# Turning attention probabilities in 32x32 blocks on VectorE, value products on four groups of 32 rows, and units of four heads

## The reference, cut to what matters

```
def sparse_attend(q, k_sel, v_sel, valid):
    s = einsum('btngd,btknd->btngk', q, k_sel) * (B_HD ** -0.5)
    s = where(valid, s, -inf)
    p = softmax(s, axis=-1)
    return einsum('btngk,btknd->btngd', p, v_sel)
```

## Time and profile before

| | us |
|---|---|
| median of three runs (lowest, highest) | 4006.8 (4002.0, 4010.1) |
| span of the profiled execution, first to last instruction | 4000.7 |
| phase of the change, first product to last copy | 2202 to 3035 |
| of it blocks 0 to 5 | 2202 to 2412 |
| of it blocks 6 to 11 | 2412 to 2749 |
| of it blocks 12 to 15 | 2749 to 3035 |

### The profile page before, as it was taken

One profiled execution on the slowest core, in us unless ns is written; L12 is line 12 of the kernel. 1 busy time (PEld: TensorE's weight loads), 2 busy tenths in 40 slices (PEclk: granted clock), 3 DMA queues, 4 the chain that ended last, 5 costly groups with the idle time before them and its releaser, 6 DMA issues. The chain is left out here.

```text
span 4000.7 us, 41769 instructions
## 1 busy us (share of the span) xinstructions
PE 3854.3 (96%) x14518; PEld 2310.1 (58%) x14518; DVE 2916.5 (73%) x3866; ACT 1411.3 (35%) x2593; POOL 1672.7 (42%) x1529
## 2 busy tenths in 40 slices
PE   7899999999999999999999799999997999999999
PEld 4555555564456566665665566555553788854444
DVE  5589999689999999999996566555454577653333
ACT  5411211155334423433431666555553322111121
POOL 0000045459687656665654332122103766552111
PEclk9999999999999999999999899999997999999999
DMA  6312222420111121211211633232232855531111
GB/s 221 92 60 65 67 87 86 142 95 37 61 61 68 50 71 64 71 63 66 72 58 59 194 120 99 70 88 77 61 102 87 226 168 171 169 128 69 40 53 46
DMA packets 290039, 368.31 MB, mean 92 GB/s; under 512 B 72635, under 2 KB 217619, under 8 KB 286630
## 3 DMA queue, kind: packets, MB, share of 16 engines
q1 hardware_dynamic: 249434, 249.73, 20.7%
q0 software_dynamic: 19664, 86.31, 5.9%
q10 hardware_dynamic: 20736, 29.66, 2.3%
HBM read 235.04 MB, written 129.28 MB: 91 GB/s over the span
## 5 line engine op out<-in xcount | busy, mean ns | idle before, releaser
L1315 DVE MAX8 best<-score 128x8 f32<-128x384 f32 (+13 forms) x448 | 639.7, 1428 | 23.3 <-POOL score L1283 8.3
L1317 DVE MATCH_REPLACE8 score<-best,score 128x384 f32<-128x384 f32 (+13 forms) x448 | 631.2, 1409 | 0.0
L1072 PE MATMUL pr<-xnT,w_row 128*128 128x347 f32 (+1 forms) x960 | 298.3, 457 | 0.0
L1224 POOL TENSOR_TENSOR kT<-kT 128x347 f32<-128x347 f32 (+1 forms) x240 | 193.8, 808 | 215.2 <-ACT kT L1142 208.4
L396 PE MATMUL pg<-xnT,wt 128*128 128x416 f32 x800 | 281.8, 515 | 0.0
L1700 PE MATMUL mix_slot<-mix_kT,mix_bq 128*128 128x512 f32 (+3 forms) x640 | 271.6, 540 | 7.7 <-DVE mix_sd L2039 3.2
L1739 PE MATMUL mix_po<-mix_probT,mix_v 128*128 128x512 f32 x544 | 240.4, 595 | 5.2 <-ACT mix_probT L1839 4.3
L1072 PEld LDWEIGHTS pr<-xnT,w_row 128*128 128x128 f32 x960 | 180.3, 190 | 106.6 <-issue 10.0
L1142 ACT COPY kT<-pr 128x347 f32<-128x347 f32 (+1 forms) x240 | 106.7, 446 | 352.9 <-PE pr L1072 342.5
L396 PEld LDWEIGHTS pg<-xnT,wt 128*128 128x128 f32 x800 | 152.6, 191 | 127.6 <-issue 127.6
L1224 POOL TENSOR_TENSOR kT<-kT,sm 128x347 f32<-128x347 f32 (+1 forms) x179 | 159.7, 892 | 124.7 <-ACT sm L1142 121.7
(11 more groups left out here) (636 smaller groups left out, 8048.0 us busy)
## 6 DMA issues: line engine op xcount, KB each, us to landing
gt_scr<-kT SPq DMA_DIRECT2D x40, 694.0 KB, 3.3
out_gm<-gt_scr ACTq DMA_DIRECT2D x32, 520.0 KB, 5.3
gt_scr<-kT SPq DMA_DIRECT2D x20, 692.0 KB, 4.2
wt<-in_w_in SPq DMA_DIRECT2D x22, 512.0 KB, 4.0
w0a<-in_w_in SPq DMA_DIRECT2D x11, 1024.0 KB, 6.6
w_row<-in_w_in SPq DMA_DIRECT2D x10, 1024.0 KB, 6.7
qt_scr<-kT POOLq DMA_DIRECT2D x8, 1040.0 KB, 4.3
early<-ybt_scr SPq DMA_DIRECT2D x4, 2080.0 KB, 9.5
```

The source lines that it names most:

```text
L1072: ins = nc.tensor.matmul(pr[:, b, 0:w], lhs, rhs, start=k == 0, stop=k == 3)
L1224: nc.gpsimd.tensor_tensor(o[:, slot, :], o[:, slot, :], term, ALU.add).then_inc(added, 1)
L1315: nc.vector.max(best[:, :], sc).then_inc(top_step, 1)
L1317: nc.vector.match_replace(sc, best[:, :], sc, TAKEN).then_inc(top_step, 1)
```

## The change

The order of the work becomes `MIX_UNITS`: 32 units of four heads (one group of keys and values) and one block, first all 16 blocks of group 0, then all 16 of group 1. Unit u has block i = u mod 16. Probabilities of several units lie in a ring of 8 x 2048 columns (`mix_ring`, `ring_places`). The events change in these ways:

- **T** is gone. A new event **X** lets DVE turn a head in blocks of 32x32 within groups of 32 rows (`nc.vector.transpose`, STREAM_TRANSPOSE). **N** leaves the reciprocal on DVE and moves the scaling to ACT.
- **O** becomes `values_times_probs`: for each 32 keys, four products of 32 rows by 128 columns, one for each group of 32 rows, each into its own bank of `mix_po` (four banks). Each product has its own weights, 32 rows of values; so the values lie in memory four times, once in each group of 32 rows (`load_values`, four transfers). There are 16(i+1) products in a unit, 4352 in all, in place of 272 of 512 columns and 1088 turns.
- PSUM: three slots of one bank in place of two slots of two and two banks for turns. Score pieces have up to 512 columns, 320 in place of 192; M2, M3 and M4 take one slot for each head; the turned keys become an event MT with a slot.
- `memory_steps` spreads the memory tile m over heads 8m-4 to 8m+3. A unit with odd i begins with M1 and MT, then M2 in two heads, then half of M3; a unit with even i has the other half of M3, M4 with Q, M4, and Y.
- The turns and products of a unit follow a unit or two later: `products(u)` turns up to unit u+1 if it is scored, then multiplies unit u. It is called when more than `ahead` units wait, or when the next unit needs ring space that a waiting one holds.
- Keys and values of group 1 are loaded in the middle of the phase, and queries and masks for every unit.

```
+        while turned <= min(u + 1, scored):
+            events.extend(("X", GQ * turned + h) for h in range(GQ))
+            turned += 1
+        events.append(("O", u))
+    scored = -1
+    for u, (kv, i) in enumerate(MIX_UNITS):
+        ahead = 2 if u == 0 or 0 < i < 6 else 1
+        while waiting and (waiting[0] <= after[u] or len(waiting) > ahead):
+            products(waiting.pop(0))
+        for h in range(GQ):
+            n = GQ * u + h
+            events.append(("S", n, 0))
+            events += memory.get(n, [])
+            if n in sample:
+                events.append(sample[n])
+            events += [("S", n, q) for q in range(1, key_pieces(n))]
+            events.append(("E", n))
+            if h:
+                events.append(("N", n - 1))
+        events.append(("N", n))
...
+                for b in range(blocks):
+                    for a in range(QUADS):
+                        rows = slice(BLK * a, BLK * a + BLK)
+                        ins = mm(po[:, a, 0:GQ * BLK], v[rows, b, :], at[rows, :, BLK * b:BLK * b + BLK], start=b == 0, stop=b == blocks - 1)
...
+                elif kind == "N":
+                    act.wait_ge(inverse, i + 1)
+                    nc.scalar.activation(probs(i), probs(i), ACT.Copy, scale=rsum[:, i % RECENT:i % RECENT + 1]).then_inc(normed, 1)
...
+                    dve.wait_ge(p_ready, i + 1)
+                    if i >= RECENT:
+                        dve.wait_ge(normed, i - RECENT + 1)
+                    nc.vector.reciprocal(rsum[:, r:r + 1], sums[:, r:r + 1]).then_inc(inverse, 1)
+                elif kind == "X":
+                    dve.wait_ge(normed, i + 1)
+                    nc.vector.transpose(probs(i), probs(i)).then_inc(turned, 1)
```

More of the change, by code:

```diff
@@ L1349, in step, with head_width, key_pieces, ring_places @@
         return 1
-def key_pieces(i):
-    return len(pieces((i + 1) * P))
-def key_groups(i):
-    return -(-(i + 1) // 4)
+GQ = BH // KV
+MIX_UNITS = [(kv, i) for kv in range(KV) for i in range(NB)]
+MIX_HEADS = GQ * len(MIX_UNITS)
+BLK = 32
+QUADS = P // BLK
+RING_COLS = 8 * SEQ
+RECENT = 8
+SLOTS = 3
 FIRST_SAMPLE_STEP = 12
 FIRST_KEYS = 4
+def head_width(n):
+    return (MIX_UNITS[n // GQ][1] + 1) * P
+def key_pieces(n):
+    return len(pieces(head_width(n), 512))
+def ring_places():
+    at, after, cursor = [], [], 0
+    for u, (_, i) in enumerate(MIX_UNITS):
+        size = GQ * (i + 1) * P
+        if cursor + size > RING_COLS:
+            cursor = 0
+        shared = [w for w in range(u) if at[w] < cursor + size and cursor < at[w] + GQ * (MIX_UNITS[w][1] + 1) * P]
+        at.append(cursor)
+        after.append(max(shared, default=-1))
+        cursor += size
+    return at, after
 def sample_events():
@@ new lines, in memory_steps @@
+def memory_steps():
+    tile = lambda m: [[("M1", m), ("MT", m)], [("M2", m, 0), ("M2", m, 1)], [("M2", m, 2), ("M2", m, 3)],
+                      [("M3", m, 0), ("M3", m, 1)], [("M3", m, 2), ("M3", m, 3)], [("M4", m, 0), ("M4", m, 1), ("Q", m)],
+                      [("M4", m, 2), ("M4", m, 3)], [("Y", m)]]
+    first = tile(0)
+    at = {n: first[2 * n] + first[2 * n + 1] for n in range(4)}
+    for m in range(1, NB):
+        for x, step in enumerate(tile(m)):
+            at[8 * m - 4 + x] = step
+    at[8 * NB - 4], at[8 * NB - 3] = [("L", 0)], [("L", 1)]
+    return at
@@ new lines, in mixing_events, with products @@
+def mixing_events():
+    sample, memory = sample_events(), memory_steps()
+    assert max(sample) < MIX_HEADS and max(memory) < MIX_HEADS
+    _, after = ring_places()
+    events, waiting, turned = [], [], 0
+    def products(u):
+        nonlocal turned
+        while turned <= min(u + 1, scored):
[18 more added lines that the diff above has]
+        events.append(("N", n))
+        waiting.append(u)
+        scored = u
+    for u in waiting:
+        products(u)
@@ L1691, in score_piece @@
             def score_piece(e):
-                _, i, hd, q = e
-                p = i % 2
-                if hd == 0 and q == 0:
-                    pe.wait_ge(a_loaded[p], 32 * (i // 2 + 1))
-                    pe.wait_ge(k_resident[i >= FIRST_KEYS], 16)
-                lo, width = pieces((i + 1) * P)[q]
-                s = take_slot(e)
-                for a, m in pieces(width, 512):
-                    ins = mm(slot[:, s, a:a + m], bq[p][:, hd, :], kT[:, hd // 4, lo + a:lo + a + m], start=True, stop=True)
@@ L1701, in score_piece @@
[L1701 to L1722 removed]
+                _, n, q = e
@@ L1922, in _ @@
                     act.wait_ge(rden_ready, i + 1)
-                    after_slot(act, ("M3", i, 0))
-                    after_slot(act, ("M3", i, 1))
+                    for hh in range(AH):
+                        after_slot(act, ("M3", i, hh))
                     for hh in range(AH):
```

414 lines of the change are left out of this document (182 added, 232 removed).

## The result

The changed kernel takes 4096.3 us (median of 4 runs, 4091.8 to 4098.4), the kernel before 4004.4 in the same comparison: a ratio of 1.0227, with a 95% interval of 1.0212 to 1.0241. It is slower by 92 us. I had forecast 4016, 9 us above the 4006.8 of its three runs then, with a range up to 4090: the sign was right and the size was not, and the time lies outside the range.

What follows compares the result with a forecast made beforehand. TensorE was taken as the bound, its order hiding the others. Blocks 0 to 5, 6 to 11 and 12 to 15 summed 179+310+353 = 842 us against 833: forecast 4016 us, 0.2% slower, range 3950 to 4090.

Steps and rivals of the forecast that it cites:

- Work that leaves and comes: TensorE: value records and turns (355 us) leave, tiled products (242) and form changes (11) come; net 102 us less.
- The other ends: Dearer prices for a set of four products on TensorE: 0.145 us (sum 73 us longer) or 0.43 (+700 us).
- The turn and the scaling: VectorE's turn 2.3 us at 2048 columns, 2.16 at 1920; ScalarE's scaling 2.01 at 2048; neither engine becomes the bound.
- Waits in the widest blocks: Blocks 12 to 15, both groups: TensorE waits 97 us in score phases and ahead of products; 353 us against 286.
- Blocks 6 to 11: Both groups: own work 281 us, waits 21 for slots and VectorE's load, 8 for gathers and drains; 310 against 337.
- Blocks 0 to 5: Both groups: own work 152 us, the 27 us of waits kept, extra value copies included in that; 179 against 210.
- The clock mis-sized: TensorE's clock drops at eight idle stretches of 7 to 12 us, 1.5 us each, 12 us in all.
- Rival 1: Waits in units 12 to 15 smaller, 55 us for 97, and 15 less elsewhere: 3950 us; chance 0.21.
- rival 2: VectorE's turn or the tiled products dearer: 4085 us at twice the turn, 4089 at 0.145 a set; chance 0.24.

Runs made afterwards that it cites:

- x6: Changed kernel with each unit placed in the ring where the latest reader is earliest, wide units at the two ends in turn: 4020.9 us.
- x2: Changed kernel with the values loaded once, in one transfer of 128 partitions, a quarter of the bytes (products read wrong blocks): 4057.1 us.
- x5: Changed kernel with all four copies kept, the rest of the values loaded two key blocks at a time behind the loads of the next units: 4069.4 us.
- x11: Changed kernel with the same four value transfers and bytes, each filling 128 partitions of a quarter of the places (products read other keys' values): 4073.5 us.
- x4: Changed kernel without the memory tiles' loads from tile 2 on, except the decay row (memory steps work on old data): 4069.6 us.
- x7: Changed kernel with a memory tile's three loads issued at three places in place of one burst, same bytes: 4064.6 us.
- x8: Changed kernel with the edits of x5, x6 and x7 together: 3968.0 us, ratio 0.9899 to the kernel before.
- x9: x8 with the sample step C moved behind its head's scores and exponential: 3953.0 us, ratio 0.9873 to the kernel before.

## Why the prediction missed, step by step

By thirds of the phase, the sum's terms and what they measured (us: length = work at full speed + idle + clock's price; the scores of units 16 and 17, which stand ahead of O15, are counted to blocks 0 to 5):

| blocks | my sum | measured |
|---|---|---|
| 0 to 5 | 179 = 152 + 27 + 0 | 267 = 170 + 73 + 23 |
| 6 to 11 | 310 = 281 + 29 + 0 | 296 = 258 + 29 + 9 |
| 12 to 15 | 353 = 249 + 92 + 12 | 359 = 250 + 86 + 24 |

**Work that leaves and comes: right.** Eight records, two for each of the four row groups, take 0.224 us in runs at the full clock, (6.53-0.27)/223 x 8 in the one below, 0.112 a set; I had 0.111.

```profile
2365.32 6.53 PE L1773 MATMUL mix_po<-mix_ring,mix_v 32*128 32x128 f32 x224
```

In sum it fell by 97 us where I had said 102; between the blocks some 20 us of it stand earlier than I had put them. The other ends that I had weighed, 0.145 and 0.43 a set, are out. The Trainium skill's factor for four row groups ("TensorE: Matmul & The Clock Gate", Part 3, Measured speedup vs the span model), 3.07, is given there for 512 columns; for the 128 columns here this trace shows more: a product of 32 rows alone would take the 0.112 of a 128-column record, so four in 0.112 are the full factor.

**The turn and the scaling: right.** VectorE's turns, and ScalarE's scaling:

```profile
L2012 DVE STREAM_TRANSPOSE mix_ring<-mix_ring 128x2048 f32<-128x2048 f32 x8 | 17.7, 2270 | 0.0
L2012 DVE STREAM_TRANSPOSE mix_ring<-mix_ring 128x1920 f32<-128x1920 f32 x8 | 16.7, 2142 | 0.0
...
L1894 ACT ACTIVATE mix_ring<-mix_ring,mix_rsum 128x2048 f32<-128x2048 f32 x8 | 15.7, 1986 | 0.0
```

I had 2.3, 2.16 and 2.01 us. One element per lane and cycle, as the Trainium skill says of the transpose ("Vector Engine (DVE) Microarchitecture Reference", 3.8), fits: (2270-2142)/128 = 1.0 ns.

**Waits in the widest blocks: right in place, and partly lucky in size.** Blocks 12 to 15 took 359 us (167 to O14's copy, 21 for O15, and 171) against 353. The four stretches ahead of the products sum to 45.6 us where I had 45, and the slots' waits stood in units 13, 15, 29 and 31. But those were 1.5 to 3.4 us each, where I had 7 to 9 for the decay factors: the score phases lost 33 us in all, sample steps included, where I had 52 (43 with the 9 that sample steps were to fill); the clock cost 24 where I had 12, and 4 us of stalls came. x6, which has no double score phase in these blocks, got 75 us back, the clock's part included.

**Blocks 6 to 11: right to 5%, by luck.** 296 us against 310, but 23 us less work and 9 for the clock, and of the 29 us of idle time, which is the figure of the sum, half (15.7) are stalls inside the products that I had not seen.

**Blocks 0 to 5: the step that failed.** I wrote "I keep the 27 us of waits" and "the extra copies of the values ... are in that". I had counted bytes, and not what the copies' transfers do on SP's queue and the DMA engines while three units need their queries and masks. In the earlier trace rows this stretch already had the highest DMA share, 0.52; that was the row to ask. The two stretches of the changed kernel show 0.62, and with the first scores of the second group they took 267 us in place of 179. TensorE's idle time there was 73 us and not 27: the two waits for masks are 30.4 of it and stalls in the products 9. Another 23 us went to the clock, and 18 us of work had been put into other blocks. x2 gives 39 us to the bytes and the way they are laid, x5 and x11 give 27 and 23 of that back without leaving a byte away.

**No term for instructions.** I priced the products by rate and not by what feeds it. 29 us of stalls in runs of products were in no step and no rival; x4 and x7 take 22 and 20 us of them away.

**The clock mis-sized.** I allowed 12 us, for the eight longest stretches. The price was 56, and 32 of it fell outside blocks 12 to 15, where I had allowed nothing (the kernel before paid 10 in its blocks 0 to 5). The granted clock was 0.5 in 28 stretches from the phase's start on, each with an idle stretch of 2.0 us or more just ahead or inside it; one wait of 2.3 us, at 2436, and some shorter ones had no fall behind them. So nearly all of the longer waits, and not eight, cost a second time. In the changed kernel and all its variants here the price is 0.29 to 0.36 of TensorE's idle time in the phase; six of them:

| kernel | phase | idle | clock's price |
|---|---|---|---|
| changed | 922 | 188 | 56 |
| x2 one copy | 888 | 155 | 49 |
| x7 memory loads apart | 892 | 159 | 48 |
| x6 two ends | 850 | 123 | 43 |
| x8 all three | 798 | 83 | 28 |
| x9 later C | 779 | 72 | 23 |

**The rivals.** None of them happened. Rival 1 had a point in the score phases of the widest blocks (33 us of waits and not 52), but the time went the other way; its own terms give 4016 - 42 - 15 = 3959, not the 3950 that I wrote. Neither turn nor products were dearer: rival 2's price, 4085 to 4089, came near the time by luck. The missing rival was one on feeding: data and instructions through the DMA engines.

## What to carry to other kernels

When an edit makes more and smaller instructions or more copies of data, price what feeds them too: the issue time on the queue, who stands behind it, the DMA share of the stretch in the profile, and the packets of instructions, which may have to wait behind a burst of loads. Waits that TensorE did not have before cost more than their length, by a third here, since the granted clock falls with them. And a buffer's place rule can set the order of a whole phase: the largest single gain (75 us) was a different place in the ring, with no instruction changed.

## What the runs showed of the hardware that I had not expected

- 512 B rows written to 32 partitions at a time: 52 ns a packet (median), 200 GB/s at a full DMA share; written to 128 partitions, 32 ns and 282 GB/s, with the same bytes (x11; the order of the rows read changed as well).
- TensorE stands still without a semaphore to wait for in fp32 products of 32 rows (4 records and 4 loads in 0.112 us), up to 7.8 us at a time, beside bursts of loads in the stretches read here, and goes on 1.20 to 1.61 us after the end of a 16 KB packet of instructions (79 of 79 stalls over 1 us, all kernels here); never, over 1 us, in the runs of 128-row products of the kernel before. That it had run dry of instructions is inferred.
- Four row groups gave the full factor of four in runs of over 200 records (0.112 us a set of four, against 0.11 for one record of 128 rows and 128 columns in the earlier trace rows).
- The profile calls a wait "issue" even where a semaphore of an engine ends it: the 10 to 13 us ahead of O12, O14, O28 and O30.
